# Hybrid encoder step: expert gates scattered into a zeroed table by adding DMAs instead of built by one-hot matmuls

## What is computed

```python
def peer_ffn(xn, w_q, sub_keys, u_tab, v_tab):            # 16384 experts = 128 x 128 keys
    q = (xn @ w_q).reshape(bsz, t, P_HEADS, 2, P_QDIM // 2)
    s = jnp.einsum('bthcd,ckd->bthck', q, sub_keys)
    sv, si = lax.top_k(s, P_TOPK)                         # 16 of 128 keys, each side
    cand = sv[..., 0, :, None] + sv[..., 1, None, :]      # 16 x 16 sums
    cand_id = si[..., 0, :, None] * N_KEYS + si[..., 1, None, :]
    top_s, top_pos = lax.top_k(cand, P_TOPK)              # 16 experts a head, 8 heads
    eid = jnp.take_along_axis(cand_id, top_pos, axis=-1)
    gate = jax.nn.softmax(top_s, axis=-1)
...
    hid = jnp.einsum('td,ted->te', xb, u_tab[eb])
    return jnp.einsum('te,ted->td', jax.nn.gelu(hid) * gb, v_tab[eb])
```

## Time and profile before

| what | us |
|---|---|
| median of three runs (lowest, highest) | 2288.07 (2275.89, 2293.09) |
| the profiled execution | 2283.04 |
| its span in the trace | 2281.2 |
| PE busy in the span | 2184.2 |
| DVE, ACT, POOL busy | 1293.3, 882.9, 924.2 |

### The profile page before, as it was taken

One profiled execution on the slowest core, in us unless ns is written; L12 is line 12 of the kernel. 1 busy time (PEld: TensorE's weight loads), 2 busy tenths in 40 slices (PEclk: granted clock), 3 DMA queues, 4 the chain that ended last, 5 costly groups with the idle time before them and its releaser, 6 DMA issues.

```text
span 2281.2 us, 41950 instructions
## 1 busy us (share of the span) xinstructions
PE 2184.2 (96%) x16703; PEld 2069.1 (91%) x16703; DVE 1293.3 (57%) x2471; ACT 882.9 (39%) x1722; POOL 924.2 (41%) x555
## 2 busy tenths in 40 slices
PE   8997888998999999999999999999979999999997
PEld 7996777888999999999999999999759999999996
DVE  4563666656798996899421111112336666666666
ACT  5235445535333333899522222222213333333332
POOL 1433344432445455211233333333765656564300
PEclk9999999898999999999999999999979999999999
DMA  3548366525666566476867677766678888888842
GB/s 129 179 135 242 92 203 190 160 84 171 183 189 193 187 189 187 154 227 218 288 238 256 234 243 239 259 227 224 227 241 275 270 276 275 271 276 269 268 150 82
DMA packets 298806, 478.86 MB, mean 210 GB/s; under 512 B 31168, under 2 KB 227584, under 8 KB 298504
## 3 DMA queue, kind: packets, MB, share of 16 engines
q1 hardware_dynamic: 276104, 409.25, 54.6%
q0 software_dynamic: 22528, 67.19, 9.5%
HBM read 383.86 MB, written 159.60 MB: 238 GB/s over the span
## 4 chain that ended last, share of the span: by engine, by line
PE 73%; DVE 2%; issue 1%; DMA 1%; ACT 1%; POOL 0%; SPq 0%; DVEq 0%; ACTq 0%; POOLq 0%
PE banks L126 22%; PE banks L128 22%; PE banks L127 22%; PE banks L2279 4%; PE banks L1968 1%; DMA u_raw<-arg_u 1%; DVE n_y L342 0%; DMA scratch_gates<-gate_stage 0%; DVE res_x L2763 0%; DVE res_lo L349 0%; DVE n_sq L383 0%; DVE n_inv L335 0%; DVE gates_in L2760 0%; ACT res_hi L1823 0%; POOL u_low L1784 0%
## 5 line engine op out<-in xcount | busy, mean ns | idle before, releaser
L126 PE MATMUL banks<-res_hi,u_high 128*128 128x288 f32 x1456 | 438.2, 301 | 2.8 <-POOL u_low L2156 1.7
L128 PE MATMUL banks<-res_hi,u_low 128*128 128x288 f32 x1456 | 428.9, 295 | 0.0
L127 PE MATMUL banks<-res_lo,u_high 128*128 128x288 f32 x1456 | 428.8, 295 | 0.0
L127 PE MATMUL banks<-w_low,v_high 128*128 128x448 f32 x1024 | 379.3, 370 | 7.7 <-issue 7.7
L126 PE MATMUL banks<-w_high,v_high 128*128 128x448 f32 x1024 | 379.4, 370 | 6.6 <-issue 6.3
L128 PE MATMUL banks<-w_high,v_low 128*128 128x448 f32 x1024 | 379.9, 371 | 5.5 <-issue 5.4
L2156 POOL TENSOR_TENSOR u_low<-u_raw,u_high 128x1024 fp32r<-128x1024 f32 x75 | 181.2, 2416 | 303.8 <-ACT u_high L2152 303.8
L2678 DVE TENSOR_TENSOR gated<-gelu_out,gates_in 128x448 f32<-128x448 f32 x76 | 48.2, 634 | 408.3 <-ACT gelu_out L2635 390.6
L126 PEld LDWEIGHTS banks<-res_hi,u_high 128*128 128x128 f32 x1456 | 273.5, 188 | 3.2 <-POOL u_low L2156 2.0
L127 PEld LDWEIGHTS banks<-res_lo,u_high 128*128 128x128 f32 x1456 | 273.6, 188 | 0.1
L128 PEld LDWEIGHTS banks<-res_hi,u_low 128*128 128x128 f32 x1456 | 273.0, 188 | 0.0
(11 more groups left out here) (424 smaller groups left out, 4594.7 us busy)
## 6 DMA issues: line engine op xcount, KB each, us to landing
scratch_v_rows<-arg_v SPq DMA_DIRECT2D x128, 512.0 KB, 8.2
v_raw<-scratch_v_rows SPq DMA_DIRECT2D x128, 512.0 KB
u_raw<-arg_u SPq DMA_DIRECT2D x37, 1024.0 KB, 5.5
scratch_gates<-gate_stage SPq DMA_DIRECT2D x14, 2048.0 KB, 7.5
scratch_prod<-gated SPq DMA_DIRECT2D x128, 224.0 KB, 3.2
w_raw<-scratch_prod SPq DMA_DIRECT2D x128, 224.0 KB
q_raw<-arg_u SPq DMA_DIRECT2D x38, 512.0 KB, 4.0
gates_in<-scratch_gates SPq DMA_DIRECT2D x19, 896.0 KB, 5.0
```

The lines of the kernel that those rows point to most:

```text
L126: pe.matmul(out, ah, bh, start=first, stop=False)
L127: pe.matmul(out, ah, bl, start=False, stop=False)
L128: return pe.matmul(out, al, bh, start=False, stop=last)
```

## The change

The gates no longer go through PE. The table of gates becomes a DRAM tensor of 128 keys x 128 x 448, which 32 stores of zeros (4 keys each, 896 KB) fill during the mixers. Then POOL adds each gate to its place by indirect DMAs with an add: one DMA moves 128 elements of 4 bytes, one from each partition, for one tile of 128 tokens and one of the 128 picks. There are 448 of them: three full tiles x 128 picks, and 64 for the last tile of 64 tokens, whose upper picks are first moved to the idle half of the partitions (`Sparse.move`). A scatter of head h waits until the scatters of the same tile of head h-1 have landed, since two heads may pick the same expert. The list `scattered_by` is all zeros, so all 448 stand on POOL's list behind its last work of routing.

```diff
+class GateRows:
+    def zero(self, sp, zeros, n):
+        k = slice(n * ZEROED, (n + 1) * ZEROED)
+        sp.dma_start(self.dst[k].rearrange("k p t -> p k t"), bc(zeros[:, :], 1, [P, ZEROED, DN])).then_inc(self.zeroed, 16)
...
+    def scatter(self, pool, h, n, k):
+        last = n == NT - 1
+        if k == 0:
+            pool.wait_ge(self.placed, h + 1)
+            if last:
+                pool.wait_ge(self.moved, 32 * (h // (P_HEADS // 2) + 1))
+            if h:
+                pool.wait_ge(self.done[n - 1], 16 * h * (TOPK // 2 if last else TOPK))
+        c = h * TOPK + k
+        pool.indirect_dma_start(
+            out=self.core.gate_rows.dst.rearrange("k p t -> (k p t)").unsqueeze(1),
+            out_offset=bass.IndirectOffsetOnAxis(ap=self.place[:, n, c:c + 1], axis=0),
+            in_=self.gates[:, n, c:c + 1], in_offset=None, compute_op=ALU.add).then_inc(self.done[n - 1], 16)
```

```diff
+                if n == NC_KEYS - 4:
+                    core.v_rows.ready(sp)
+                    sparse.scattered(sp)
...
+                        load_w(sp, k)
+                        load_v(sp, k)
...
+        def out_key(dve, k):
+            if k == 0:
+                weigh_key(dve, 0)
+            split_v_low(dve, k)
+            if k + 1 < N_KEYS:
+                weigh_key(dve, k + 1)
+            for s in range(rows_due(k - 1), rows_due(k)):
+                accumulate(dve, s)
+            split_w_low(dve, k)
...
         def dve_hidden(dve):
+            dve.wait_ge(u.low, 2)
+            for n in range(2, NC_KEYS):
+                u.split_low(dve, n // JJ, n % JJ)
+                if n >= NC_KEYS - PRE:
+                    out_key(dve, n - NC_KEYS + PRE)
```

- A row gather no longer waits for the third before it to land; it waits until PE is within 8 keys (`AHEAD_ROWS`) of the key at which its row is added (keys 10 to 121):

```diff
             def row(s):
                 if s >= RING:
                     pool.wait_ge(summed_rows, s - RING + 1)
-                if s >= IN_FLIGHT:
-                    landed(s - IN_FLIGHT)
+                if ROW_KEY[s] > AHEAD_ROWS:
+                    pool.wait_ge(out_done, ROW_KEY[s] - AHEAD_ROWS)
```

More of the change, by code:

```diff
@@ L225, in __init__ @@
         self.ready = core.sem("picks_by_row")
+        self.placed = core.sem("picks_placed")
+        self.moved = core.sem("picks_moved")
+        self.done = [core.sem(f"gates_scattered{n}") for n in range(1, NT)]
+        self.order = []
+        for h in range(P_HEADS):
+            self.order += [(h, n, k) for n in range(1, NT - 1) for k in range(TOPK)]
+            if h >= P_HEADS // 2:
+                self.order += [(h - P_HEADS // 2, NT - 1, k) for k in range(TOPK // 2)]
+        self.order += [(h, NT - 1, k) for h in range(P_HEADS // 2, P_HEADS) for k in range(TOPK // 2)]
@@ L228, with scattered @@
+    def scattered(self, eng):
+        for n in range(1, NT):
+            eng.wait_ge(self.done[n - 1], 16 * P_HEADS * (TOPK // 2 if n == NT - 1 else TOPK))
 class Gemm:
@@ L1021, in out_loads, with copy_and_zero @@
                         sp.dma_start(raw_ahead[:, c + 1], a["w_out"][c]).then_inc(core.wout_loaded[c], 16)
+                def copy_and_zero(n):
+                    core.v_rows.copy(sp, MIX_COPIES[n], MIX_COPIES[n + 1])
+                    for z in range(8 * n, 8 * n + 8):
+                        core.gate_rows.zero(sp, zeros, z)
                 rows_gone(sp)
@@ L1881, in route_jobs, with route @@
     return jobs + [("hidden", n) for n in range(h, AHEAD4)]
-def route(core, norm, gemm, jobs, sel, numbers, keys, gelu, gelu_sent, sel_out, sparse):
+def route(core, norm, gemm, jobs, numbers, keys, gelu, gelu_sent, sparse, u):
     nc, a = core.nc, core.a
@@ L1958, in pool_route, with pe_route @@
                     match_keys(*match_after[j])
-            spread.first_low(pool)
-        def pe_route(pe, spread):
+                for h, n, k in sparse.order[scattered_by[j - 1]:scattered_by[j]]:
+                    sparse.scatter(pool, h, n, k)
+            for n in range(2):
+                u.split_low(pool, 0, n)
+            for h, n, k in sparse.order[scattered_by[LAST]:]:
+                sparse.scatter(pool, h, n, k)
+        def pe_route(pe):
             def scores(c):
@@ L2093, in place_picks @@
-                dve.tensor_copy(sparse.expert[:, :], left[:, 1, :]).then_inc(sparse.ready, 1)
-                dve.tensor_copy(sparse.hidden[:, :], left[:, 2, :]).then_inc(sparse.ready, 1)
-                dve.tensor_copy(sparse.gate[:, :], picks[:, 0, 2, :]).then_inc(sparse.ready, 1)
+                link(dve.tensor_reduce(column[:, 0, :], own, AX_X, ALU.add))
+                for n in range(1, NT):
+                    ins = dve.tensor_scalar(column[:, n, :], column[:, 0, :], 1.0, float((n - 1) * P), ALU.mult, ALU.add)
@@ new lines, in number_tokens, with place_rows @@
+                link(ins)
+            def place_rows():
+                e, f = left[:, 1, :], left[:, 2, :]
+                link(dve.scalar_tensor_tensor(out=e, in0=picks[:, 0, 1, :], scalar=float(N_KEYS), in1=picks[:, 0, 0, :],
+                                              op0=ALU.mult, op1=ALU.add))
+                link(dve.tensor_scalar(f, e, float(SP), column[:, 0, :], ALU.mult, ALU.add))
+                dve.tensor_copy(sparse.expert[:, :], e).then_inc(sparse.ready, 1)
+                dve.tensor_copy(sparse.hidden[:, :], f).then_inc(sparse.ready, 1)
@@ L2427, in experts, with rows_due @@
-def experts(core, acts, u, project, route, spread, sparse, ring, total, gelu_sent_ahead, mixing_sems):
+ACC_FROM, ACC_TO = 10, 122
+AHEAD_ROWS = 8
+def rows_due(k):
+    return min(SEL, max(0, (k - ACC_FROM + 1) * SEL // (ACC_TO - ACC_FROM)))
+ROW_KEY = [next(k for k in range(N_KEYS) if rows_due(k) > s) for s in range(SEL)]
+def experts(core, acts, u, project, route, sparse, ring, total, gelu_sent_ahead, gemm, mixing_sems):
     nc, a = core.nc, core.a
```

536 lines of the change are left out of this document (133 added, 403 removed).

## The result

The changed kernel takes 2518.45 us (2510.24 to 2521.09, 4 runs) where the kernel before takes 2287.74 (2275.89 to 2293.09, 4 runs): ratio 1.101, interval 1.096 to 1.106. I had forecast 2317, +1.3%. The direction was right and the size was not; the result lies at the top end of my range of 8 in 10 (2220 to 2520) and far outside the forecast's own range (2275 to 2360). The profiled execution took 2519.8 us, with a span of 2518.0.

What follows compares the result with a forecast made beforehand. PE, busy 96%, was taken as the bound. The scatter wait takes back the 104.8 us won: second layer at 1604.5, + 634.9 + 55 + 15.3 = 2309.7 of span, forecast 2317 us against 2288; own range 2275 to 2360, 8 in 10: 2220 to 2520.

Steps and rivals of the forecast that it cites:

- The scatters: POOL behind routing: 448 scatters at the gather's 0.94 us plus 0.30, from 921, all landed by 1577.5.
- rival 3: Scatters on POOL or in DMA: adding costs more than a gather; 2432 at 1.7 us, 2557 at 1.98; chance 0.34.
- DVE's hold: First layer: DVE's 1024-column subtraction lengthens the scatter beside it from 0.94 to 1.94 us, once a key.
- Rival 1: First layer: DVE's subtraction does not hold POOL; scatters keep 1.245 us, landing by 1489; time 2228; chance 0.13.
- The landings: Last four groups of 8 scatters: each waits 2.2 us for the one before, less what is hidden: +8.
- Where PE stops and for what: First layer: PE stops before key 88 at 1481.6 until the scatters land; second layer starts 27 us after landing.
- The second layer: From 1604.5: 128 keys at 4.96 us, 634.9, plus 55 for DMA.
- The +55 for DMA: Second layer: 0.229 MB more a key at 290 GB/s makes 5.45 us a key, over 112 keys; bounds 0 and +96.
- rival 2: Second layer: DMA gives 319 GB/s, so 55 us fall away and the time is 2262; chance 0.12.
- The rush: Start of second layer, 1620 to 1690: back-to-back row gathers, now paced by PE, so 31.9 us go.
- The key's period: Second layer: 4.96 us a key as in its even part before, 634.9 us for 128 keys.
- The mixers: Zeros written in the mixers, 29 MB against 36 MB of copies saved: taken as 0, between -5 and +10 us.

Runs made afterwards that it cites:

- the first experiment: Changed kernel with all 448 scatters writing instead of adding, so doubles keep one gate: 2177.87 us, 0.969 of the kernel before; on another chip 2756.61 us, 1.206.
- the paced kernel before: Kernel before, with row gathers held by PE's finished keys (at most 8 ahead) instead of the third gather before landing: 2241.28 us, ratio 1.001.
- the first two experiments: Changed kernel with plain writes instead of adds (2177.87 us, 0.969), and with only heads 0 to 3 scattered, 224 of 448 (2152.76 us, 0.958).
- The joined one: Changed kernel with DVE adding up doubled gates, plain scatters, 48 of them in routing: 2169.94 us, 0.966 of before; on another chip 2659.35 us, 1.163.
- The spaced one: Joined-gates kernel with DVE's last two low halves of u first, plus a 128-column POOL fill before each scatter: 2265.34 us, 0.992 of before.
- the two spaced kernels: Joined-gates kernel, later DVE order, with a POOL fill before each scatter: 128 columns 2265.34 us; 16 columns 2305.87 to 2441.64 us.

## Why the forecast was wrong, step by step

- **The scatters: this term failed.** I sized them by the gather's row, 0.94 us; the adding scatter takes 1.547. My ends of the range had room for it (1.98 us a cycle; measured 1.70 + 0.30 = 2.0), and rival 3 had 0.34, but the sum and the forecast went by the gather's row, for which I had no more than that it was the nearest. At its dear end rival 3 had the wait's end (1818) and, without the error in the second layer, nearly the time. SP's loads started at 1833.2 where I had 1577.5, 255.7 us later. The plain scatters (0.96 us) show that it is the adding, and not the direction. By parts: 448 x (1.547 - 0.94) = +272; the start at 927.4 in place of 921, +6; DVE's hold 66.5 in place of one us in each of 88 keys, -21. They add up to 257.
- **DVE's hold** was right in kind, 0.8 us once a key and not 1.0. Rival 1 is contradicted for this adding scatter, since the hold disappears with the subtraction, and so is what the Trainium skill infers ("SBUF — State Buffer", "Who interferes with whom"). My "gather beside it" was too coarse: only a scatter that begins inside a subtraction is held. All but 3 of the plain ones in the first experiment took 0.95 to 1.00 us, because those that met it began ahead of it.
- **The landings**: 2.2 us a group forecast whole, 8 hidden in part; measured 8.9 us for the groups. Right.
- **Where PE stops and for what**: in front of key 88, for DVE's low half of u behind SP's loads, at 1487.6 (forecast 1481.6), at half clock. Right. From the loads to the second layer it took 33.8 us and not 27; 5.2 of the 6.8 are a second stop, in front of key 89, that the sum left out.
- **The second layer: this term failed too**, and hid a fifth of the first error. Forecast 689.9, measured 1866.99 to 2502.6, 635.6: 54 us less. The +55 for DMA does not exist (rival 2, and the Trainium skill's 358 GB/s in "DMA: Bandwidth & Descriptors", "Where 436 GB/s comes from", came nearer than my row: 322 to 329 GB/s here with PE full, up to 377 in windows on another chip, above that figure). I had read 290 GB/s beside a slow PE as cause, and it was effect: PE was slow for another reason, so fewer loads were asked for (5 of w and 5 of v in the 50 us from 1640, and 21 of each in the 100 us from 1900). The row that shows it, "issue" in front of each matmul, stood in the trace of before; and ACT's 18.35 us in rows 6, which I took for a late w, end in "remote", which names no load.
- **The rush** was expected to go wholly (-31.9); with paced row gathers some 13 us of it stayed (635.6 less 128 x 4.86). From 1889 to 1901 PE starts matmuls mostly 1.4 us apart, each wait ending in "issue", while POOL issues value and row gathers 1.25 us apart. Right in direction, through starving and not through late loads. It is no accident of one execution: in the eleven profiles with paced gathers from the chips where before takes 2277 to 2288 us the second layer is 4 to 14 us longer than 128 of its own usual keys, and in the eight from the other two chips, paced or not, 0 to 1.
- **The key's period**: 4.96 us before, 4.86 after. Both appear with either kernel (the paced kernel before has 4.86; of the first two experiments, on one chip, one has 4.86, the other 4.96). It isn't the change's, and what sets it is open. Here it gave 12 us.
- **The mixers**: routing's first matmul is at 548.8 here, but at 541.4 and 541.5 in the other two profiled executions of the changed kernel, and at 542.7 before. The zeros cost less than this spread; their price alone wasn't tried. From there to routing's last matmul it is 378.0 us here, and 379.3 before with 1.3 us of transposes in it, so DVE's added operations in routing cost nothing, as I had it.

Sum: 2309.7 + 255.7 + 6.8 (restart) - 54.3 = 2517.9, against a span of 2518.0.

What the case doesn't settle: why PE starves. Shown is that it comes with indirect DMAs that start 1.2 to 1.4 us apart, on the chips where before takes 2277 to 2288 us, that the profile then shows nothing that PE waits for, and that with a fill that makes the mean 1.60 us it is gone. On the chips of 2238 and 2246 it wasn't seen at 1.27. It would account for most of that difference of some 45 us in the kernel before: 31.9 of rush, and 12.8 more if the period was the slower one on the first chip only. That is argued, since there is no trace of the kernel before from those chips. The kernel before with paced gathers was not run on a chip that starves.

The best version depends on the chip. The joined one takes 0.966 of before where PE doesn't starve and 1.163 where it does. The spaced one, 0.992 on a starving chip, is the only version with all its gates that wasn't slower on such a chip, and its gain is under 1%; it wasn't run on the other kind.

## What to carry to other kernels

An operation that no row shows deserves a run of its own before a change is built on 448 of it; the nearest row is a guess about kind, and here the adding made an indirect DMA 1.6 times as long, at both sizes tried. Where hundreds of operations of one engine stand in front of a wait, its length times their count is the forecast: look for the mean at which the wait starts to bind (here 1.25 us). And before a slow stretch of PE is put down to late data, read what ended the idle time before its matmuls: "issue" is not a load.

## What the runs showed of the hardware

- An adding indirect scatter of 128 elements of 4 bytes takes POOL 1.547 us, a plain one 0.96, a gather 0.94, each with 0.30 to the next; with 64 elements 1.41 and 0.89. On a starving chip the plain ones grow to 1.09 and 1.10 us, of either size.
- An indirect DMA that begins inside a DVE subtraction of 1024 columns (1.23 us) is held until 0.13 us before its end: the adding one takes 2.35 so in nearly every key, a gather 1.94, a plain scatter 1.47 and 1.85 in the two spaced kernels. One that has begun before the subtraction isn't held (86 of them in the run with adding scatters of 64 elements, 81 in the first experiment).
- Indirect DMAs 1.2 to 1.4 us apart made PE start a matmul only every 1.4 to 2.1 us on the first chip and every 2.8 us on three others, at half clock (with DMA down to 8 GB/s over 440 us); two chips showed nothing of it with the same code at 1.27. At means of 1.60 us and more (1.80 for the adding ones of 64, 2.02 for those of 128) it was absent.
- DMA moved 322 to 329 GB/s over most of the second layer with PE full, and 377 over 20 us on another chip, one core at work.
